# Attention's output projection: one full float32 product against three float32r products of split operands

## What is computed

```python
mix = jnp.concatenate([sb_out, d_out.astype(sb_out.dtype)], axis=-1)   # 512 x 1024
x = x + mix @ w_o[layer]                                               # 1024 x 1024
h2 = rmsnorm(x, ffn_norm_g[layer])
x = x + (jax.nn.silu(h2 @ w_gate[layer]) * (h2 @ w_up[layer])) @ w_down[layer]
```

## Time and profile before

| | us |
|---|---|
| median of 3 runs | 2592.58 (2592.16 to 2596.48) |
| the profiled execution | 2584.88, its span 2582.9 |
| stretch in question | 160 to 366 of the span |

### The profile page before, as it was taken

How to read it: one execution, slowest core, us unless ns; L and a number is a source line. 1 busy time by engine, 2 the same in 40 slices (tenths; PEclk the granted TensorE clock), 3 DMA queues, 4 the chain that set the end, 5 groups by cost and what they waited for, 6 DMA issues and landing times.

```text
span 2582.9 us, 41027 instructions
## 1 busy us (share of the span) xinstructions
PE 2439.0 (94%) x17615; PEld 1537.2 (60%) x17615; DVE 1607.1 (62%) x1749; ACT 820.6 (32%) x1361; POOL 405.0 (16%) x423
## 2 busy tenths in 40 slices
PE   8998899999989999999979989999999999999996
PEld 6765468888779898989879973333323323232322
DVE  4335456665437898989485641666666666666664
ACT  3255544444344645464454421000000000000001
POOL 0024011212101312122430400100000000011110
PEclk9999999999999999999989998999999999999998
DMA  5200068878755454546523367899999999999996
GB/s 201 82 33 1 25 234 286 294 284 287 271 198 186 154 184 154 189 148 205 171 93 132 153 261 298 353 410 413 413 414 411 412 412 414 413 412 413 410 416 233
DMA packets 129717, 676.31 MB, mean 262 GB/s; under 512 B 19300, under 2 KB 52068, under 8 KB 100228
## 3 DMA queue, kind: packets, MB, share of 16 engines
q1 hardware_dynamic: 56624, 554.81, 54.1%
q0 software_dynamic: 25632, 88.49, 10.1%
q10 hardware_dynamic: 47284, 30.42, 4.3%
HBM read 618.55 MB, written 55.12 MB: 261 GB/s over the span
## 4 chain that ended last, share of the span: by engine, by line
PE 65%; DMA 19%; DVE 8%; ACT 4%; issue 2%; POOL 1%; ACTq 0%; POOLq 0%; DVEq 0%
PE PS L1151 24%; PE PS L837 11%; DMA expert_ring_high<-w_experts 11%; PE PS L1019 4%; DMA arena<-w_proj 3%; PE PS L783 3%; PE PS L779 3%; PE PS L780 3%; PE PS L1024 2%; DMA expert_ring_low<-w_experts 2%; DMA ring<-ssd_sums 2%; ACT ring L1558 2%; PE PS L683 1%; PE PS L634 1%; PE PS L630 1%
## 5 line engine op out<-in xcount | busy, mean ns | idle before, releaser
L1151 PE MATMUL PS<-expert_ring_high,U 128*32 128x512 f32 x4240 | 470.4, 594 | 16.9 <-DMA expert_ring_high<-w_experts 16.1
L1151 PE MATMUL PS<-expert_ring_low,U 128*32 128x512 f32 x4016 | 451.6, 597 | 11.2 <-DMA expert_ring_low<-w_experts 9.1
L837 PE MATMUL PS<-XH,RINGF 128*128 128x264 f32 x2304 | 392.3, 289 | 1.2 <-ACT arena L1502 1.2
L1151 PEld LDWEIGHTS PS<-expert_ring_high,U 128*32 128x32 f32 x4240 | 135.3, 110 | 327.0 <-issue 301.4
L837 PEld LDWEIGHTS PS<-XH,RINGF 128*128 128x128 f32 x2304 | 324.2, 189 | 9.2 <-issue 6.8
L1151 PEld LDWEIGHTS PS<-expert_ring_low,U 128*32 128x32 f32 x4016 | 128.9, 111 | 314.5 <-issue 293.9
L2339 DVE SCALAR_TENSOR_TENSOR arena<-expert_ring_low,U,arena 128x2048 f32<-128x2048 f32 x134 | 305.7, 2345 | 0.0
L837 PE MATMUL PS<-UH,RINGF 128*128 128x264 f32 x1152 | 233.5, 285 | 0.0
L2072 DVE SCALAR_TENSOR_TENSOR H<-arena,par,H 128x528 f32<-128x528 f32 x240 | 186.6, 821 | 1.3
L837 PEld LDWEIGHTS PS<-UH,RINGF 128*128 128x128 f32 x1152 | 179.1, 189 | 0.0
L2339 DVE SCALAR_TENSOR_TENSOR arena<-expert_ring_high,U,arena 128x2048 f32<-128x2048 f32 x76 | 174.0, 2347 | 0.5
(11 more groups left out here) (358 smaller groups left out, 3871.5 us busy)
## 6 DMA issues: line engine op xcount, KB each, us to landing
expert_ring_low<-w_experts SPq DMA_DIRECT2D x96, 2048.0 KB, 26.8
expert_ring_high<-w_experts SPq DMA_DIRECT2D x96, 2048.0 KB, 30.6
arena<-w_proj POOLq DMA_DIRECT2D x72, 512.0 KB, 5.6
projection_low_parts<-PREL POOLq DMA_DIRECT2D x72, 512.0 KB, 4.3
ring<-w_proj SPq DMA_DIRECT2D x72, 512.0 KB, 3.6
RINGF<-projection_low_parts SPq DMA_DIRECT2D x72, 512.0 KB, 4.6
ring<-w_gu SPq DMA_DIRECT2D x11, 2048.0 KB, 10.4
ring<-ssd_sums ACTq DMA_DIRECT2D x32, 512.0 KB, 8.4
```

Of the source, the lines that this page charges most:

```text
L837: last = nc.tensor.matmul(PS[:, banks[i], 0:HT], w[:, k, :], x[:, k, lo:hi], start=start, stop=stop)
L1151: mm = nc.tensor.matmul(PS[QUAD * t:QUAD * t + QUAD, bank, :], stat(t), move(t), start=start, stop=stop)
```

## The change

`wo` becomes three float32r products. Its weights are split in the stick-breaking stage, one tile of 128x1024 for each head: ACT copies the high part of tile i-1 ahead of its wait for the mask, DVE subtracts the low part at the end of its turn, in place over the weights. The high parts lie where the input projection's weight pieces were, so ACT waits for the last of those products. The input `MIX` is split in two parts: k 0 to 3 in the last differential head (ACT's copies at steps 12 to 15, DVE's subtractions at steps 13 to 16), k 4 to 7 behind ACT's last root, DVE's subtractions between and behind the multiplications with the roots. PE now waits for each tile's `weights_low` and, in `wo(0)`, for `x_low` of each k; it no longer waits for `mix_ready` nor for the weights' arrival. POOL's and SP's programs are unchanged.

The core of the diff:

```diff
             def wo(m, ks):
-                name = ("wo", m // 4)
-                w = slot(name)
+                hi, lo = wo_high(m), wo_low(m)
                 if ks.start == 0:
+                    pe.wait_ge(S("weights_low"), WO_W + m + 1)
                     open_(("wo", m), m % 4)
                 for k in ks:
-                    last = nc.tensor.matmul(PS[:, m % 4, :], w[:, k, (m % 4) * P:(m % 4) * P + P], MIX[:, k, :],
-                                            start=(k == 0), stop=(k == DT - 1))
+                    if m == 0:
+                        pe.wait_ge(S("x_low"), MIX_X + k + 1)
+                    nc.tensor.matmul(PS[:, m % 4, :], hi[:, k, :], mix_high(k), start=(k == 0), stop=False)
+                    nc.tensor.matmul(PS[:, m % 4, :], hi[:, k, :], mix_low(k), start=False, stop=False)
+                    last = nc.tensor.matmul(PS[:, m % 4, :], lo[:, k, :], mix_high(k), start=False, stop=(k == DT - 1))
...
             for m in range(DT):
-                if m in (0, 4):
-                    arrived(("wo", m // 4))
                 if m < 4:
                     subln_sum(m)
                 wo(m, range(0, 4 if m < 4 else DT))
                 if m == 3:
-                    pe.wait_ge(S("mix_ready"), DIFF_HEADS)
                     for j in range(4):
                         wo(j, range(4, DT))
...
                 if i >= 1:
+                    name = ("wo", (i - 1) // 4)
+                    act.wait_ge(S(f"ring{slot_of[where[name]]}"), landed[name])
+                    act.wait_ge(*in_used[23])
+                    A(wo_high(i - 1), wo_raw(i - 1), ACT.Copy).then_inc(S("weights_high"), 1)
                     act.wait_ge(S("arg_masked"), i)
                     A(Z(i - 1), Z(i - 1), ACT.Exp).then_inc(S("w_ready"), 1)
...
+                if 12 <= n < 16:
+                    got(act, ("s", 11))
+                    act.wait_ge(*freed(("o", 2 * (n - 12) + 1)))
+                    A(mix_high(n - 12), MIX[:, n - 12, :], ACT.Copy).then_inc(S("x_high"), 1)
...
-            act.wait_ge(S("mix_ready"), DIFF_HEADS)
+            got(act, ("do", DIFF_HEADS - 1))
+            for h in range(DIFF_HEADS):
+                act.wait_ge(S("mix_ready"), h + 1)
+                A(mix_high(4 + h), MIX[:, 4 + h, :], ACT.Copy).then_inc(S("x_high"), 1)
...
                 if i >= 2:
                     stick_out(i - 2)
+                if i >= 1:
+                    dve.wait_ge(S("weights_high"), WO_W + i)
+                    V_.tensor_tensor(wo_low(i - 1), wo_raw(i - 1), wo_high(i - 1).bitcast(F32), SUB).then_inc(S("weights_low"), 1)
...
+            def mix_rest(k):
+
+                dve.wait_ge(S("x_high"), MIX_X + k + 1)
+                V_.tensor_tensor(mix_low(k), MIX[:, k, :], mix_high(k).bitcast(F32), SUB).then_inc(S("x_low"), 1)
...
+                if 13 <= n < 17:
+                    mix_rest(n - 13)
             for h in range(DIFF_HEADS):
                 dve.wait_ge(S("head_rooted"), 8 + h + 1)
                 R = QK[:, h, :]
                 V_.scalar_tensor_tensor(MIX[:, 4 + h, :], MIX[:, 4 + h, :], small[:, 5:6], R, MUL, MUL).then_inc(S("mix_ready"), 1)
+                if h >= 1:
+                    mix_rest(4 + h - 1)
+            mix_rest(4 + DIFF_HEADS - 1)
```

More of the change, by code:

```diff
@@ L104 @@
 assert N_PRE_WO + sum(PRE_GATE) + len(PRE_DOWN) == N_PROJ
-FFN_W = 24
+WO_W = 24
+FFN_W = WO_W + DT
 PROJ_W = FFN_W + 2 * FFT + 32
@@ L109 @@
 FFN_USED, TAIL_USED = 6, 30
-GX_X = 2 * DT
+MIX_X, FFN_X = DT, 2 * DT
+GX_X = FFN_X + DT
 U_X = GX_X + FFT
@@ L281, in program, with mix_high, mix_low, wo_raw @@
         SUMMED = U[:, 4, 0:3 * P]
+        rows = GX[:, :, :, :].rearrange("p a f n -> p (a f) n")
+        MIX_ROW, V_ROW, QK_ROW = 17, 9, 1
+        assert 2 * DT * SEQ + (FBUF + STAGE) * PIECE - DT * T2 == P + 5 * 1280 + (16 - V_ROW) * SEQ
+        def mix_high(k):
+            return rows[:, (2, 3, 5, 6)[k] if k < 4 else V_ROW + k - 4, :]
+        def mix_low(k):
+            return rows[:, MIX_ROW + k, :]
+        def wo_raw(m):
+            return slot(("wo", m // 4))[:, :, (m % 4) * P:(m % 4) * P + P]
+        def wo_high(m):
+            return WI[:, m // 4, m % 4, :].rearrange("p (k n) -> p k n", k=DT)
+        def wo_low(m):
+            return RINGF[:, slot_of[where["wo", m // 4]] - 2, :].rearrange("p (k n) -> p k n", k=DT)[:, :, (m % 4) * P:(m % 4) * P + P]
         def Z(h):
@@ L748, in wo @@
             def wo(m, ks):
-                name = ("wo", m // 4)
-                w = slot(name)
+                hi, lo = wo_high(m), wo_low(m)
                 if ks.start == 0:
+                    pe.wait_ge(S("weights_low"), WO_W + m + 1)
                     open_(("wo", m), m % 4)
                 for k in ks:
-                    last = nc.tensor.matmul(PS[:, m % 4, :], w[:, k, (m % 4) * P:(m % 4) * P + P], MIX[:, k, :],
-                                            start=(k == 0), stop=(k == DT - 1))
+                    if m == 0:
[3 more added lines that the diff above has]
+                    last = nc.tensor.matmul(PS[:, m % 4, :], lo[:, k, :], mix_high(k), start=False, stop=(k == DT - 1))
                 if ks.stop == DT:
                     fill(last, ("wo", m))
-                    last_read[name] = ("wo", m)
+                    last_read[("wo", m // 4)] = ("wo", m)
             for m in range(DT):
-                if m in (0, 4):
-                    arrived(("wo", m // 4))
                 if m < 4:
@@ L777, in split_piece @@
                     if p == 0:
-                        pe.wait_ge(S("x_low"), DT + k + 1)
+                        pe.wait_ge(S("x_low"), FFN_X + k + 1)
                     nc.tensor.matmul(PS[:, bank, :], hi[:, k, :], src[:, 0, k0 + k, :], start=(start and k == 0), stop=False)
@@ L1960, in _ @@
                 if m >= 1:
-                    x_low("ffn_g", m - 1, DT)
+                    x_low("ffn_g", m - 1, FFN_X)
                     if m >= 2:
```

## The result

| | before | after |
|---|---|---|
| median of the runs (us) | 2592.22 (2589.43 to 2599.68, 8 runs) | 2599.70 (2598.79 to 2610.98, 8 runs) |
| the profiled execution, its span | 2584.88, 2582.9 | 2610.98, 2608.9 |

The changed kernel is slower: the ratio is 1.0033 (95% interval 1.0017 to 1.0049), 7.5 us in the medians. That is more than the 0.2% at which the forecast drew the line between same and slower, though the interval reaches down to 0.17%, and it is above the forecast range (2585 to 2597). The profiled execution of after is 11 us above its own median, so the time is read by stretches between landmarks that both kernels have, and a second profile of the same kernel (e1_again) stands beside it.

The account below looks back on a forecast made before the run. Up to the gate stage the preload tiles' path (last x_low at 357.8), not PE's (353.8), sets the end. Tile path -3.3 us plus clock +2.4 gave -0.9: median 2591.7 us, range 2585 to 2597.

Parts of the forecast that it names:

- the weight split's zero: Stick-breaking heads: ScalarE's copies and VectorE's subtractions fit into idle time, cost 0; without this cover 8.5 and 9.8 us.
- rival C: Stick-breaking heads: subtractions hold up GpSimd and through it PE, at most 9.8 - 0.9 us slower, 2601.5; chance 0.05.
- The products: Output projection on PE: 54.9 us removed, 43.8 added at 0.2283 us per product, 11.1 us less on PE alone.
- ScalarE's copies at zero: Stick-breaking heads: eight weight copies of 1.057 us fit where ACT idles 2.44 us per head, cost 0.
- The first half of the input split: Last differential head: ACT's copies and VectorE's subtractions delay the first norm sum by 0.7 us, bounds 0 and 1.3.
- The tile path: Preload tiles up to the last x_low: sets the end; tile 3 lands at 333.7 and all behind it 3.3 us earlier.
- The clock's 2.5 for 2.4: Start of the gate stage: PE waits, its clock falls and costs 2.4 us, bounds 0 and 2.7.
- A: Preload: gate weights don't hold up tile 3; 5.4 us less, 2587.2, or 2584.8 with the clock kept; chance 0.12.
- B: Output projection: PE's path was the real bound, so 8.7 us less, 2583.9; chance 0.05.
- the second sets the end: Kernel before, gate start: PE's path ends at 353.8, tile 5's at 357.8, and the latter sets the end.
- D: Preload: tile 3 lands no earlier (336 or 337) and the clock is lost; +1.5 to +2.4 us, 2594 to 2595; chance 0.17.
- E: Output projection: three passes not cheaper, so no gain on PE at all; excluded beforehand, no chance given.

Follow-up runs that it names:

- e1_again: The changed kernel word for word, run and profiled a second time: 2598.93 us, ratio 1.0027 to the kernel before.
- e2: Changed kernel with VectorE's weight subtractions waiting until GpSimd's masks and mostly its sums of that head are done: 2589.68 us, ratio 0.9998 to before.
- e3: Changed kernel with each weight subtraction cut to 1 of 128 columns and the third product reading the high part: 2590.68 us, ratio 0.9993 to before.
- e4: Changed kernel with each weight subtraction replaced by a one-input maximum of the same size and place: 2592.21 us, ratio 0.9996 to before.
- e12: The kernel of e2 once more, word for word: 2592.07 us, ratio 0.9998 to the kernel before.
- e6: Kernel of e2 with three of six preload tiles moved from the output projection to the gate stage: 2592.33 us, ratio 0.9995 to before.
- e7: Kernel before with three of six preload tiles moved from the output projection to the gate stage: 2603.01 us, ratio 1.0041 to before.

## Why the prediction was wrong

**The step that failed** is the weight split's zero, and in it the sentence "one subtraction is 1.22 and starts as the masks end". It priced only what the subtraction does to GpSimd's three sums, where PE has 1.6 us of slack; for the masks' end PE waits with none (masks to 197.97, PE from 198.02 in that head), and that wait it had at nothing. By its own figure, 197.8, the subtraction already began 0.17 us ahead of the masks' end. And it read one head of two kinds: every other one has the subtraction start 0.36 us ahead, and there the masks end 1.49 us late and PE with them. The trace of before had both kinds. It also had the row of a held mask, and the prediction named the mechanism as rival C, with a chance of 0.05; but the point of decision it gave ("pushed by more than 1.6 us") belongs to the sums and not to the masks. e2, e3 and e4 each take the loss away in another way and leave ScalarE's copies and the order of the rest in place, so this cause is shown. Where exactly a mask begins to be held is not.

**Its size.** C gave at most 9.8 us, eight times 1.22. Measured against e2 the first two stretches are 11.4 us longer in after and 10.6 in e1_again, from four in-head losses and the one behind the heads; three subtractions cost nothing. It is above that bound because a held mask costs up to 1.49 and because the clock is added: PE's idle time grows by 5.0 us in the heads, and 3.2 are the clock that falls on such waits, a term that the prediction counted at the gate stage (the earlier trace rows show it) but not here.

**What was right.** The products: in the stream of `wo` one starts every 0.23 us. ScalarE's copies at zero (e3). The first half of the input split: 0.2 us in e2, forecast 0.7 with 0 as a bound. The tile path as the bound, to 0.6 us, with tile 3 landing just when it was forecast. The clock's 2.5 for 2.4. In e2, which is the change without the failed step, the first four stretches sum to 197.5 us against 200.0 before, 2.5 shorter, and in its repeat e12 to 198.6, 1.4 shorter, where 0.9 were forecast; the medians can't tell it from none, as the forecast said of the whole.

**The rivals.** A (tile 3 isn't held up) is refuted by 9.34 and 9.06 us beside the gate weights and 5.44 without them; the prediction took from the Trainium skill ("DMA: Bandwidth & Descriptors", section on queues, rings and completion order) that a small transfer wouldn't wait for a large one, and found the trace against it. That page of the Trainium skill states only that each DMA engine takes a packet from each queue in turn. The trace agrees with that (54 packets against 66 from 340 to 343), and since SP's packets are more than three times as large, GpSimd's transfers are slowed by it. B (PE alone was the bound) is refuted by the measured 57.8 to 58.0 and by e6, where the stretch shrinks when tiles leave it. But e7 shows that PE's path, with the `x_low` behind it, was level with that of the tiles in before: without the three tiles nothing is gained there (62.5). So the prediction's "the second sets the end" was half right for the kernel before. D (no gain on the tile path) is refuted by the same 58.0. E is refuted by the products.

## What to carry to other kernels

Before an instruction of VectorE with two operands in SBUF is put into an idle gap, lay its start and end over GpSimd's timeline, and for each GpSimd instruction that it touches or comes near ask who waits for that one's end: a start 0.36 us ahead of the masks' end cost 1.49 us here, one 0.24 us behind their undisturbed end still 1.6, and since PE waited for it, the clock on top. Do it for every head or turn of the loop, not for one: two kinds alternated here. Such work is free where the other engine is idle (here 3 us later in the same head), or in a form with one operand. An engine that gets faster and then waits may give the gain back by its clock; some products that nobody reads, fitted so that they end before the awaited data, kept it here.

## What was not expected of the hardware

- One VectorE instruction of 1.2 us with two SBUF operands made a GpSimd mask of 0.29 us last 1.78 (eight masks 5.25 against 3.70 to 3.76 us) where it began 0.36 us ahead of the masks' end, and left the last mask as it was where it began 0.13 ahead. It also held a mask that would have ended 0.24 us ahead of its recorded start (four masks 2.63 us instead of 1.03). One with one operand, of 1.2 us and at the same places, held up nothing (3.70 and 1.03).
- The granted clock stayed at 1.00 for nearly 5 us in which PE worked 1.81 (359 to 364); it was at 0.60 in the next two and at 0.50 from 366 to 368, with PE busy again. In the heads it fell behind a gap of 1.48 us in one (208 to 220) and not in another of the same length (at 235.81 the 14 products took 3.09).
- 21 products that do nothing were worth about 0.3% (interval 0.17% either way) in two kernels that wait there, where the profiled stretch accounts for 0.1%.
